# w_lo of early and of gates chunks made on VectorE, query copies ahead of a weight chunk, and a causal softmax without its scaling step in a one-core two-block transformer kernel

## What is computed

```python
h = _rms_norm(x, g_pre_mix[l])
proj = h @ w_in[l]
qa, ka, va, c_q, c_kv, k_r, gate_logits = _split_cols(proj, ...)
...
o_a = _moba_attention(qa, ka, va).reshape(B, S, MOBA_WIDTH) @ w_branch_a[l]
...
o_b = _mla_attention(q_nope, q_rope, k_nope, k_rope, v_b).reshape(B, S, MLA_WIDTH) @ w_branch_b[l]
gates = jax.nn.sigmoid((gate_logits + b_gate[l]).astype(jnp.float32)).astype(x.dtype)
merged = gates[..., :D_MODEL] * o_a + gates[..., D_MODEL:] * o_b
```

## Time and profile before

| | us |
|---|---|
| median of 3 runs | 836.79 (835.68 to 839.15) |
| the profiled execution's own time | 836.71 |
| its span | 834.9 |
| PE busy | 801.7 (96%) |
| DVE / ACT / POOL busy | 417.1 / 419.7 / 389.1 |

### The profile page before, as it was taken

One profiled execution on the slowest core, in us unless ns is written; L12 is line 12 of the kernel. 1 busy time (PEld: TensorE's weight loads), 2 busy tenths in 40 slices (PEclk: granted clock), 3 DMA queues, 4 the chain that ended last, 5 costly groups with the idle time before them and its releaser, 6 DMA issues.

```text
span 834.9 us, 14259 instructions
## 1 busy us (share of the span) xinstructions
PE 801.7 (96%) x5477; PEld 698.0 (84%) x5477; DVE 417.1 (50%) x673; ACT 419.7 (50%) x643; POOL 389.1 (47%) x186
## 2 busy tenths in 40 slices
PE   5999998999899999999999999999999999999996
PEld 3678876887578999999998889899987988999885
DVE  4566566983747332333236648454454434323435
ACT  5335424463665544444444954555755654444543
POOL 3446000000053566546653987545554564566552
PEclk9999999999999999999999999999999999999998
DMA  9884567135843655665654788343445555656651
GB/s 319 285 274 134 171 232 248 51 105 180 249 131 111 209 172 184 193 194 165 188 182 131 209 201 207 96 136 102 152 160 168 154 189 187 201 176 182 189 157 50
DMA packets 94396, 146.61 MB, mean 176 GB/s; under 512 B 15747, under 2 KB 64112, under 8 KB 94352
## 3 DMA queue, kind: packets, MB, share of 16 engines
q1 hardware_dynamic: 92896, 143.23, 55.3%
q0 software_dynamic: 1424, 2.77, 1.2%
q10 hardware_dynamic: 32, 0.01, 0.0%
HBM read 144.93 MB, written 1.06 MB: 175 GB/s over the span
## 4 chain that ended last, share of the span: by engine, by line
PE 85%; DVE 7%; ACT 3%; issue 2%; DMA 2%; POOL 1%; DVEq 0%; SPq 0%; ACTq 0%
PE bank L1846 82%; DMA ctx_rows<-in_ctx 1%; POOL w_lo L621 1%; PE bank L2109 1%; DVE w_lo L1176 1%; DMA raw<-in_w_in 1%; ACT w_hi L679 1%; DVE stat L1491 1%; PE bank L2407 1%; DVE mod_cols L1217 1%; DVE x L1798 1%; DVE probs L1451 0%; DVE h_f L1227 0%; DVE h_lo L1236 0%; DVE bank L1539 0%
## 5 line engine op out<-in xcount | busy, mean ns | idle before, releaser
L621 POOL TENSOR_TENSOR w_lo<-raw,w_hi 128x1024 fp32r<-128x1024 f32 (+2 forms) x155 | 374.0, 2431 | 288.3 <-ACT w_hi L679 269.1
L679 ACT ACTIVATE w_hi<-raw 128x1024 fp32r<-128x1024 f32 (+1 forms) x218 | 226.2, 1045 | 223.3 <-PE bank L1846 196.5
L1176 DVE TENSOR_TENSOR w_lo<-raw,w_hi 128x1024 fp32r<-128x1024 f32 x66 | 81.2, 1239 | 147.3 <-ACT w_hi L679 147.0
L1846 PE MATMUL bank<-z_hi,w_hi 128*128 128x256 f32 x384 | 108.7, 283 | 0.0
L1846 PE MATMUL bank<-z_hi,w_lo 128*128 128x256 f32 x384 | 107.4, 280 | 0.0
L1846 PE MATMUL bank<-z_lo,w_hi 128*128 128x256 f32 x384 | 107.1, 279 | 0.0
L1846 PE MATMUL bank<-n_hi,w_hi 128*128 128x256 f32 x352 | 99.5, 283 | 0.5 <-DVE n_lo L1581 0.5
L1846 PE MATMUL bank<-n_lo,w_hi 128*128 128x256 f32 x352 | 99.1, 282 | 0.0
L1846 PE MATMUL bank<-n_hi,w_lo 128*128 128x256 f32 x352 | 99.0, 281 | 0.0
L1846 PE MATMUL bank<-w_hi,mlp_h_hi 128*128 128x512 f32 x216 | 85.5, 396 | 0.0
L1846 PE MATMUL bank<-w_hi,mlp_h_lo 128*128 128x512 f32 x216 | 85.3, 395 | 0.0
(11 more groups left out here) (409 smaller groups left out, 1596.9 us busy)
## 6 DMA issues: line engine op xcount, KB each, us to landing
raw<-in_w_in SPq DMA_DIRECT2D x54, 512.0 KB, 4.5
raw<-in_w_down SPq DMA_DIRECT2D x54, 512.0 KB, 3.8
raw<-in_w_gu SPq DMA_DIRECT2D x44, 512.0 KB, 3.6
raw<-in_w_mod SPq DMA_DIRECT2D x32, 512.0 KB, 4.3
raw<-in_w_up SPq DMA_DIRECT2D x32, 512.0 KB, 3.7
raw<-in_w_mod SPq DMA_DIRECT2D x32, 256.0 KB, 5.9
raw<-in_w_out SPq DMA_DIRECT2D x12, 512.0 KB, 3.9
raw<-in_w_in SPq DMA_DIRECT2D x8, 336.0 KB, 2.9
```

The source lines that it names most:

```text
L621: nc.gpsimd.tensor_tensor(wl[:, w % SPL, 0:size], raw[:, slot_raw, 0:size], wh[:, w % SPL, 0:size].bitcast(F32), ALU.subtract).then_inc(s_ ...
L679: nc.scalar.activation(wh[:, w % SPL, 0:size], raw[:, slot_raw, 0:size], ACT.Copy).then_inc(s_hi, 1)
L1176: V.tensor_tensor(wl[:, w % SPL, :], raw[:, slot_raw, :], wh[:, w % SPL, :].bitcast(F32), ALU.subtract).then_inc(s_lod, 1)
L1846: return nc.tensor.matmul(out_, l, r_, start=start, stop=stop, skip_group_check=True)
```

## The change

It has six parts. (1) `by_dve` names chunks 1, 2, 5 and 6 of the front too: DVE makes their w_lo in modulation(1) and modulation(3), between the copy of the rows and the bias. (2) In the levels ACT copies queries and rows b before the w_hi of chunk 21 instead of behind it, and makes the w_hi of chunk 22 after level_keys(3). (3) The `hg mean` copies go from hg_tail(7) to hg_tail(8) on ACT. (4) In the setup of the causal attention PE transposes rT before mT, and mT in the order 0, 2, 1, 3; ACT copies qrT, mT 0 and mT 1 with the attention's scale in the copy, and DVE copies krT, mT 2 and mT 3; the first scores wait for mT 0 and mT 2 alone. (5) The scale being in the queries, the maximum comes negated out of the reduction, and L1714 goes. (6) `by_dve` names the gates chunks 3, 5, 7, 9, 11, 13 and 15, and in steps 0 to 6 DVE makes the w_lo of gates chunk 2m + 3 behind `cprobs(2m + 1)`, ahead of o_lo(0) and of the gates copies. `flat` joins neighbouring tiles into one row; N1 and N1W number the second block's first chunk.

```diff
             c1, c2 = w - W0, w - M0W
-            return (w == 0 or 12 <= w < W_END["g"] + 2 or c1 == 3 or (4 <= c1 < 4 + 12 * MLP1_TRIPS and (c1 - 4) % 6 >= 4)
-                    or w == W_END["out"] - 1 or w in (W2["branch a"] - 1, W2["branch b"] - 3, W2["branch b"] - 1) or c1 == 5 + 12 * MLP1_TRIPS or c2 == 3 + 12 * MLP2_TRIPS or c2 in (-2, -1) or (2 <= c2 < 2 + 12 * MLP2_TRIPS and (c2 - 2) % 12 in (2, 3, 8, 9)))
+            return (w in (0, 1, 2, 5, 6) or 12 <= w < W_END["g"] + 2 or c1 == 3 or (4 <= c1 < 4 + 12 * MLP1_TRIPS and (c1 - 4) % 6 >= 4)
+                    or w == W_END["out"] - 1 or (W2["ukv"] + 3 <= w < W2["gates 3"] and (w - W2["ukv"]) % 2) or w in (W2["branch a"] - 1, W2["branch b"] - 3, W2["branch b"] - 1) or c1 == 5 + 12 * MLP1_TRIPS or c2 == 3 + 12 * MLP2_TRIPS or c2 in (-2, -1) or (2 <= c2 < 2 + 12 * MLP2_TRIPS and (c2 - 2) % 12 in (2, 3, 8, 9)))

...
             level_keys(2)
-            hi(22)
+            hi(21)
             act.wait_ge(s_used, W_END["q"])
...
             nc.scalar.activation(rowb[:], ps[0][:], ACT.Copy).then_inc(AC.sem, AC.tick("rows b"))
+            hi(22)
+            level_keys(3)
             hi(23)
-            level_keys(3)
             act.wait_ge(AC.sem, AC["q 1"])
...
                         nc.scalar.activation(xn[:, 0, 512 * j:512 * j + 512], ps[6 + j][:], ACT.Square).then_inc(AC.sem, AC.tick(f"hg sq {j}"))
-                elif n == 7:
+                elif n == 8:
                     for j in range(2):
...
             for j in range(2):
-                nc.scalar.activation(flat(qnT, 2 * j, 2), ps[6 + j][:], ACT.Copy).then_inc(AC.sem, AC.tick(f"qnT {j}"))
+                nc.scalar.activation(flat(qnT, 2 * j, 2), ps[6 + j][:], ACT.Copy, scale=96 ** -0.5).then_inc(AC.sem, AC.tick(f"qnT {j}"))
             hi2(26)
...
                 nc.scalar.activation(flat(knT, 2 * j, 2), ps[j][:], ACT.Copy).then_inc(AC.sem, AC.tick(f"knT {j}"))
-            hi2(27)
             for t in range(2):
                 nc.scalar.activation(vb[:, t, :], ps[2 + t][:], ACT.Copy).then_inc(AC.sem, AC.tick(f"vb {t}"))
+            hi2(27)
+            act.wait_ge(PE.sem, PE["rT"])
+            nc.scalar.activation(flat(qrT, 0, 2), ps[0][:], ACT.Copy, scale=96 ** -0.5).then_inc(AC.sem, AC.tick("qrT"))
+            for b in (0, 1):
+                act.wait_ge(PE.sem, PE[f"mT {b}"])
+                nc.scalar.activation(flat(mT, 2 * b, 2), ps[MT_BANKS[b]][:], ACT.Copy, scale=HD ** -0.5).then_inc(AC.sem, AC.tick(f"mT {b}"))
             hi2(28)
-            for b in range(4):
-                act.wait_ge(PE.sem, PE[f"mT {b}"])
-                nc.scalar.activation(flat(mT, 2 * b, 2), ps[MT_BANKS[b]][:], ACT.Copy).then_inc(AC.sem, AC.tick(f"mT {b}"))
-            act.wait_ge(PE.sem, PE["rT"])
-            nc.scalar.activation(flat(qrT, 0, 2), ps[0][:], ACT.Copy).then_inc(AC.sem, AC.tick("qrT"))
-            nc.scalar.activation(krT[:], ps[1][:, 0:T], ACT.Copy).then_inc(AC.sem, AC.tick("krT"))

...

-                scale = HD ** -0.5 if n < 8 else 96 ** -0.5
                 act.wait_ge(DV.sem, DV[f"cmax {n}"])
...
                     nc.scalar.activation(pc[:, n % 2, c0:c1], ps[n % 2][:, c0:c1], ACT.Exp, bias=stat[:, 128 + 2 * n + t:129 + 2 * n + t],
-                                         scale=scale, accum_out=stat[:, 160 + 2 * n + t:161 + 2 * n + t]
+                                         accum_out=stat[:, 160 + 2 * n + t:161 + 2 * n + t]
                                          ).then_inc(AC.sem, AC.tick(f"cexp {n} {t}"))
...

-            def modulation(g):
+            def modulation(g, lows=()):

...
                 tick(V.tensor_copy(modrow[:, g % 2, :], ps[6][:]), f"row {g}")
+                for w in lows:
+                    chunk_lo(w, number["w"][w] % RAW)
                 dve.wait_ge(PE.sem, PE[f"mod t {g}"])
...
             for g in (1, 2):
-                modulation(g)
+                modulation(g, (1, 2) if g == 1 else ())
                 h_pair(g)
...

-            modulation(3)
+            modulation(3, (5, 6))
             h_pair(3)
...
                 tick(V.tensor_copy(kr4[:, t], qr[:, t, 8:9, :].broadcast_to([P, 4, 32])), f"kr4 {t}")
+            dve.wait_ge(PE.sem, PE["rT"])
+            tick(V.tensor_copy(krT[:], ps[1][:, 0:T]), "krT")
+            for b in (2, 3):
+                dve.wait_ge(PE.sem, PE[f"mT {b}"])
+                tick(V.tensor_copy(flat(mT, 2 * b, 2), ps[MT_BANKS[b]][:]), f"mT {b}")

...

-                scale = HD ** -0.5 if n < 8 else 96 ** -0.5
                 dve.wait_ge(PE.sem, PE[f"cs {n}"])
-                V.tensor_reduce(stat[:, 128 + 2 * n:129 + 2 * n], ps[n % 2][:, 0:P], AX, ALU.max)
-                done(V.tensor_reduce(stat[:, 129 + 2 * n:130 + 2 * n], ps[n % 2][:, P:384], AX, ALU.max), f"cm {n}")
-                done(V.tensor_scalar(stat[:, 128 + 2 * n:130 + 2 * n], stat[:, 128 + 2 * n:130 + 2 * n], -scale, None, ALU.mult), f"cmax {n}")
+                V.tensor_reduce(stat[:, 128 + 2 * n:129 + 2 * n], ps[n % 2][:, 0:P], AX, ALU.max, negate=True)
+                tick(V.tensor_reduce(stat[:, 129 + 2 * n:130 + 2 * n], ps[n % 2][:, P:384], AX, ALU.max, negate=True), f"cmax {n}")

...
                 cprobs(2 * m + 1)
+                if m < 7:
+                    w = W2["ukv"] + 3 + 2 * m
+                    chunk_lo(w, (N1 + w - N1W) % RAW)
                 if m == 5:
...
             gates_chunk(0)
-            pe.wait_ge(DV.sem, DV["qr"])
-            pe.wait_ge(AC.sem, AC["vb 1"])
-            for b in range(4):
-                for c in range(4):
-                    m = 2 * b + c // 2
-                    ins = nc.tensor.transpose(ps[MT_BANKS[b]][:, P * c:P * c + P], mqk[:, c % 2, P * m:P * m + P], ident)
-                ins.then_inc(PE.sem, PE.tick(f"mT {b}"))
-
+            pe.wait_ge(AC.sem, AC["knT 1"])
             pe.wait_ge(DV.sem, DV["kr4 1"])
-            pe.wait_ge(AC.sem, AC["vb 1"])
             for c in range(4):
...
             ins.then_inc(PE.sem, PE.tick("rT"))
+            pe.wait_ge(AC.sem, AC["vb 1"])
+            for b in (0, 2, 1, 3):
+                for c in range(4):
+                    m = 2 * b + c // 2
+                    ins = nc.tensor.transpose(ps[MT_BANKS[b]][:, P * c:P * c + P], mqk[:, c % 2, P * m:P * m + P], ident)
+                ins.then_inc(PE.sem, PE.tick(f"mT {b}"))

...
                 if m == 0:
-                    pe.wait_ge(AC.sem, AC["krT"])
+                    pe.wait_ge(AC.sem, AC["mT 0"])
+                    pe.wait_ge(DV.sem, DV["mT 2"])
                 else:
...
                 if m == 0:
-                    pe.wait_ge(AC.sem, AC["mT 3"])
+                    pe.wait_ge(AC.sem, AC["mT 1"])
                 if m == 4:
```

## The result

The changed kernel takes 844.47 us (median of 7 runs, 840.03 to 845.71). The kernel before took 835.68 us in the 7 runs beside them (834.55 to 839.3). The ratio is 1.0084 with a 95% interval of 1.0061 to 1.0106, so the change costs about 7 us by the ratio; the two medians lie 8.8 us apart. The predicted 838.3 us lies under the measured median, and so does the whole range up to 840.7.

What follows compares the result with a forecast made beforehand. PE was taken as the bound, busy 801.7 of 834.9 us. The terms -2.0 - 4.4 + 0.5 - 1.3 + 7.3 + 1.5 = +1.6 us on 836.71 gave 838.3 us; 8-in-10 range 832.3 to 840.7.

Steps and rivals of the forecast that it cites:

- Part 6, the waits: Causal loop steps 1, 3 and 5: new PE waits of 2.15, 1.3 and 3.8 us, costing 7.3 us.
- longer than the 2.93 after which the clock was at its lower level for 3 us, so 1.5 more: Behind causal step 5: the wait of 4 us lowers PE's clock, costing 1.5 us more.
- the rival of three falls: Causal steps 1, 3 and 5: clock falls behind all three waits; 841.3 us, chance 0.10.
- Part 2: Between levels 2 and 3: PE's 2.93 us wait and the half clock behind it go; gain 4.4 us.
- Parts 1, 4 and 5: Front: two PE waits go, gain 2.0 us; causal setup: gain 1.3; dropping L1714: nothing.
- Part 3: First attention, step 4: chunk 26's w_hi still precedes the exponentials, PE's wait shrinks about 0.1 us; cost 0.5.
- Not held: Causal loop: DVE's w_lo is not held by POOL's, part 6 costs 3.2 us; 832.8 us, chance 0.15.
- hidden: Causal loop: the w_lo on DVE costs PE nothing; 829.5 us, chance 0.10.
- one wait of 2.18 us without a fall: First attention, step 4: no lower clock followed this wait, so waits in steps 1 and 3 cost none.

Runs made afterwards that it cites:

- part 6 alone: The kernel before with only part 6 of the change added; 847.27 us, ratio 1.012.
- fed_wait_8: The changed kernel with 8 matmuls of unused result on PE ahead of its wait for o_lo in step 5; 840.29 us, ratio 1.0047.
- part 2 alone: The kernel before with only part 2 of the change added; 834.45 us, ratio 0.9975.
- both_on_vectore: The changed kernel, but in steps 1 to 6 DVE makes both gates w_lo and GpSimd none; 838.17 us, ratio 1.002.
- hg_mean_before_again: The changed kernel with DVE's w_lo behind o_lo(0) and the gates copies, and part 3 undone; 832.59 us, ratio 0.9931.

## Why the prediction was wrong, step by step

- **Part 6, the waits: right, in place, cause and size.** 2.15, 1.3 and 3.8 us were predicted, 2.1, 1.2 and 3.9 came, for the reason given: the w_lo is bound to the second w_hi, held by GpSimd's and ahead of o_lo and the gates copies.
- **The step that failed: "longer than the 2.93 after which the clock was at its lower level for 3 us, so 1.5 more."** I took the length of the stretch from the only one that the trace before had. Behind 4.04 us it was 10 us in the changed kernel and about 7 in the kernel with part 6 alone, and it cost 3.9 us in the trace of the changed kernel and 3.1 to 4.2 by fed_wait_8. With the right size the sum is 840.7, at the end of my range, and this is the term that the range and the rival of three falls (1.5 us for each) also had too small.
- **Part 2: right in the trace, too large for the median.** The wait and its half clock went, 4.7 us. But part 2 alone is worth 2.1 us: the wait of 2.93 us was one draw, and the other trace of the same code has 0.79. All five other parts together give 5.4 us where 7.2 was predicted. This error and that of the clock go the same way: with 5.4 and with part 6 at 11.1 the kernel before at 836.7 gives 842.4, and with part 6 at the 12.4 of the ratios 843.7. What is left to 844.47 is not placed.
- **Parts 1, 4 and 5: right as far as the traces tell.** Part 1 gives 1.3 to 2.0 for 2.0, parts 4 and 5 together 1.5 for 1.3. No run has one of them alone.
- **Part 3: the mechanism right, the size not measurable.** ACT waits for chunk 26's data instead of the copies, and PE's wait stays. Moving that w_hi is what took 2.6 us, though a wait and a stretch at half clock came up behind it.
- **The rivals.** "Not held" and "hidden" fall by the rows of steps 1 and 5 and by both_on_vectore. The clock did not fall behind the waits of 2.0 and 1.1 us in steps 1 and 3, in any of the five traces with them. But the reason that the prediction gave, one wait of 2.18 us without a fall, was a draw: hg_mean_before_again has a wait of 2.18 us at that same place (212.96) and half clock right behind it.
- **What the two traces add.** Of their 7.8 us, about 2 (half clock at 20 us) and 1.4 (first MLP) are not of the change, as the last section shows.

## What to carry to other kernels

Before an instruction that waits for another engine is put into a queue, read what stands behind it and who waits for that: the same seven w_lo cost 1.3% of the kernel ahead of o_lo and the gates copies, and nothing behind them. Price a new wait of TensorE as the wait plus the clock behind it, and take from the traces a range for the second, not the one stretch that is there; work of no use in the wait gives the second part back. A wait that ends with a DMA is a draw: a single trace shows one of its values, so its removal is priced from the runs' median, or with both ends.
